# Hybrid mLSTM and attention encoder layer: the input projection and the memory stage become one stage

## The reference, cut to what matters

```
h = rmsnorm(x) * norm_pre
q_m, k_m, v_m, o_m, z_m, if_raw, q_a, k_a, v_a, z_a, g_m, g_a = split(h @ w_in)
for both directions, head by head:              # the memory, as one product over the whole sequence
    b = cumsum(log_sigmoid(f)); a = i - b; m = running max of a (and 0)
    s[t, u] = (q_t . k_u) / 16 * exp(a_u - m_t)  for u up to t (from t on, backwards)
    h_dir[t] = sum_u s[t, u] v_u / max(|sum_u s[t, u]|, exp(-(b + m)_t))
y_m = ((h_fwd + h_bwd) * sigmoid(o_m) * silu(z_m)) @ w_mo
y_a = (attention(rope(q_a), rope(k_a), v_a) * silu(z_a)) @ w_ao
y = rmsnorm(x + (sigmoid(g_m) * y_m + sigmoid(g_a) * y_a) @ w_out) * norm_final
```

## Time and profile before

| | us |
|---|---|
| median of three runs (lowest, highest) | 2832.71 (2832.28, 2835.37) |
| span of the profiled execution, first to last instruction | 2828.9 |
| PE busy, share of the span | 2482.5, 88% |
| DVE, ACT, POOL busy | 1286.5, 884.5, 1064.5 |
| projection's products, gates, memory, all after it | 1265.0, 44.9, 431.9, 1048.1 |

### The profile page before, as it was taken

How to read it: one execution, slowest core, us unless ns; L and a number is a source line. 1 busy time by engine, 2 the same in 40 slices (tenths; PEclk the granted TensorE clock), 3 DMA queues, 4 the chain that set the end, 5 groups by cost and what they waited for, 6 DMA issues and landing times. The chain is left out here.

```text
span 2828.9 us, 31968 instructions
## 1 busy us (share of the span) xinstructions
PE 2482.5 (88%) x11236; PEld 1999.2 (71%) x11236; DVE 1286.5 (45%) x1882; ACT 884.5 (31%) x1564; POOL 1064.5 (38%) x771
## 2 busy tenths in 40 slices
PE   6999999999999999994577776499599888968998
PEld 5888888888888888883455454378477776756887
DVE  6111111112111111103799997489489787862332
ACT  4111111111111111112344332334488776862121
POOL 4111111112211111100567564355377666756320
PEclk9999999999999999997798988699799999998999
DMA  4322222222222222110434332488622323115332
GB/s 157 119 75 75 74 89 75 75 75 89 75 100 78 89 75 75 53 60 20 143 113 151 102 112 89 163 282 281 203 81 81 113 73 97 35 43 204 109 141 90
DMA packets 182207, 299.33 MB, mean 106 GB/s; under 512 B 14864, under 2 KB 72720, under 8 KB 182080
## 3 DMA queue, kind: packets, MB, share of 16 engines
q1 hardware_dynamic: 145520, 225.29, 24.0%
q10 hardware_dynamic: 36560, 72.45, 7.0%
HBM read 190.41 MB, written 107.25 MB: 105 GB/s over the span
## 5 line engine op out<-in xcount | busy, mean ns | idle before, releaser
L148 DVE CAST a_w_hi<-a_raw 128x512 fp32r<-128x512 f32 (+1 forms) x152 | 170.8, 1194 | 995.1 <-PE a_acc L165 995.1
L154 POOL TENSOR_TENSOR a_w_lo<-a_raw,a_w_hi 128x512 fp32r<-128x512 f32 (+1 forms) x160 | 219.6, 1406 | 983.0 <-DVE a_w_hi L148 983.0
L163 PE MATMUL a_acc<-a_act_hi,a_w_hi 128*128 128x512 f32 x1368 | 533.1, 390 | 0.0
L164 PE MATMUL a_acc<-a_act_lo,a_w_hi 128*128 128x512 f32 x1368 | 532.7, 389 | 0.0
L165 PE MATMUL a_acc<-a_act_hi,a_w_lo 128*128 128x512 f32 x1368 | 532.7, 389 | 0.0
L202 ACT ACTIVATE a_stage<-a_acc 128x512 f32<-128x512 f32 x228 | 136.2, 598 | 1081.3 <-PE a_acc L165 1081.3
L1500 POOL TENSOR_TENSOR t_prob<-t_prob,t_rsum 128x1024 f32<-128x1024 f32 (+1 forms) x192 | 308.2, 1609 | 134.8 <-DVE t_rsum L1520 134.8
L164 PEld LDWEIGHTS a_acc<-a_act_lo,a_w_hi 128*128 128x128 f32 x1368 | 257.2, 188 | 53.4
L165 PEld LDWEIGHTS a_acc<-a_act_hi,a_w_lo 128*128 128x128 f32 x1368 | 257.1, 188 | 53.4
L163 PEld LDWEIGHTS a_acc<-a_act_hi,a_w_hi 128*128 128x128 f32 x1368 | 257.3, 188 | 53.1
L1579 PE MATMUL t_scr<-t_k,t_q 128*128 128x512 f32 x640 | 185.0, 404 | 43.8 <-DMA t_k<-stacks 23.8
(11 more groups left out here) (179 smaller groups left out, 4102.8 us busy)
## 6 DMA issues: line engine op xcount, KB each, us to landing
p_feat<-a_stage ACTq DMA_DIRECT2D x42, 1024.0 KB, 4.2
a_raw<-w_in SPq DMA_DIRECT2D x19, 2048.0 KB, 7.7
stacks<-r_flat SPq DMA_DIRECT2D x12, 1536.0 KB, 7.3
p_tok<-a_stage ACTq DMA_DIRECT2D x15, 1024.0 KB, 4.2
m_raw_kq<-p_feat SPq DMA_DIRECT2D x24, 512.0 KB, 5.4
t_q<-stacks SPq DMA_DIRECT2D x8, 1536.0 KB, 6.4
t_k<-stacks SPq DMA_DIRECT2D x16, 768.0 KB, 8.5
r_x<-p_tok SPq DMA_DIRECT2D x12, 768.0 KB, 4.9
```

The source lines that it names most:

```text
L148: nc.vector.tensor_copy(g.w_hi[:, slot, k, 0:width], g.raw[:, k, 0:width]).then_inc(g.hi_split[slot], 1)
L154: nc.gpsimd.tensor_sub(g.w_lo[:, slot, k, 0:width], g.raw[:, k, 0:width], g.w_hi[:, slot, k, 0:width].bitcast(F32)).then_inc(g.lo_split[sl ...
L163: nc.tensor.matmul(out, stat_hi(k), mov_hi(k), start=(k == 0), stop=False)
L164: nc.tensor.matmul(out, stat_hi(k), mov_lo(k), start=False, stop=False)
```

## The change

- The projection keeps the split input in an outer scope and multiplies only 10 blocks of 512 and the gates' block: q and k (4), v (2), attention's q, k, v (3), and one block made of the first head's halves of `o_m` and `z_m`. The gates' work runs inside, between the third to fifth blocks, on five tiles of 128 by 1024, with the two sequences and directions on four groups of partitions.
- q, k and v leave it already split: ACT copies the high part out of PSUM, DVE subtracts for the low part, and both are stored (`kq`, `vs`).
- The other 36 blocks of 128 columns (`o_m` and `z_m` of three heads, `z_a`, `g_m`, `g_a`: 108 groups) are multiplied in the memory's stage, one group every 0.755 tick, from two PSUM tiles. ACT splits their weights (high) and POOL (low), ACT takes them out with Sigmoid or Silu.
- The memory has 80 units in one unrolled order. It loads q, k and v split. A unit's values follow 1.45 ticks after its scores, from weights that are not scaled; the two directions have PSUM sums of their own, and a chunk's numerators are multiplied once by the inverse denominator. The denominator is made as columns (8 matmuls of one column), inverted, and spread by 8 transposes on PE. Three POOL operations end a chunk: add the directions, two gatings.
- A unit in which both directions meet now has values in two pieces of (j+1) and (4-j) blocks of 128 columns, six matmuls each.
- The pre-loaded semaphores of these stages become plain counts, and one setting of the program, the room for dynamic transfers, is made 1024.

The core of the diff (removed lines of the old stages left out; they are printed above):

```diff
-    project(nc, x, w_in, norm_pre, p_feat, p_tok, gate_rows)
-    prepare_gates(nc, gate_rows, b_if, neg_max, floor, a_cols)
-    mlstm(nc, p_feat, p_tok, neg_max, floor, a_cols, scratch("inverse", NDIR * CH), g_mem)
+    project_and_remember(nc, x, w_in, norm_pre, b_if, gate_rows, kq, vs, p_tok, p_feat, neg_max, g_mem)
...
+A_UNITS = [("qk", C_QM, 0), ("if", C_IF, 0), ("qk", C_QM + UNIT, 1), ("qk", C_QM + 2 * UNIT, 2),
+           ("qk", C_QM + 3 * UNIT, 3), ("v", C_VM, 0), ("v", C_VM + UNIT, 1), ("tok", C_QA, S_QA),
+           ("tok", C_QA + UNIT, S_QA + UNIT), ("tok", C_KVA, S_KVA), ("oz", C_OM, 0)]
...
+                    if kinds[idx] in ("qk", "v"):
+                        nc.scalar.activation(stage[:, i % 2, 0, j, :].bitcast(F32R), a[:], ACT.Copy).then_inc(half_made, 1)
...
+                        nc.vector.tensor_sub(stage[:, i % 2, 1, j, :].bitcast(F32R), acc[(G0[idx] + n) % NB][:],
+                                             stage[:, i % 2, 0, j, :]).then_inc(lo_made, 1)
...
+    for u, (_, _, _, j, _) in enumerate(units):
+        at("sp", u - 1.9, "load k", u)
+        at("sp", u - 1.0, "load v", u)
+        if j is not None:
+            at("dve", u - 0.75, "argument", u)
+        at("act", u - 0.6, "decay", u)
+        at("pe", u, "scores", u)
+        at("dve", u + 0.2, "weigh", u)
+        at("pool", u + 0.4, "sum", u)
+        at("act", u + 0.55, "high", u)
+        at("dve", u + 0.65, "low", u)
+        at("pe", u + 1.45, "values", u)
+    for ch in range(len(first)):
+        a, z = first[ch], last[ch]
+        at("sp", a - 2.6, "load q", ch)
+        at("sp", a - 2.5, "load nmax", ch)
+        at("pool", a + 0.35, "zero", ch)
+        at("sp", z - 1.0, "load gates", ch)
+        at("pe", z + 1.25, "den", ch)
+        at("act", z + 1.3, "abs", ch)
+        at("dve", z + 1.4, "invert", ch)
+        at("pe", z + 1.65, "spread", ch)
+        at("act", z + 1.75, "norm", ch)
+        at("dve", z + 1.9, "out", ch)
+        at("pool", z + 2.1, "gate", ch)
+        at("sp", z + 2.6, "store out", ch)
+    for g in range(NG_B):
+        t = -1.0 + g * 0.755 + 0.07
+        at("pe", t, "group", g)
+        at("act", t + 0.6, "drain", g)
+        at("sp", t + 1.0, "store group", g)
+        if g % NCH == 0:
+            i = g // NCH
+            at("sp", t - 2.9, "load w", i)
+            at("act", t - 1.5, "w high", i)
+            at("pool", t - 1.4, "w low", i)
...
+                elif kind == "drain":
+                    act.wait_ge(acc_full, n + 1)
+                    if n >= 3:
+                        act.wait_ge(stored[n % 3], 16 * (n // 3))
+                    nc.scalar.activation(stage[:, n % 3, :], acc[n % 2][:], ZG_SUBS[n // NCH][2]).then_inc(drained, 1)
...
+                    for d, out in ((1, out_f), (0, out_b)):
+                        ins = nc.vector.tensor_mul(out[:], num[d][:], norm[:, d:d + 1, :].to_broadcast([P, 2, CH]))
+                    ins.then_inc(out_read, 1)
...
+                    nc.gpsimd.tensor_add(out_f[:], out_f[:], out_b[:]).then_inc(gate_step, 1)
+                    pool.wait_ge(gate_step, 2 * n + 1)
+                    nc.gpsimd.tensor_mul(out_f[:], out_f[:], gate_o[:]).then_inc(gate_step, 1)
+                    pool.wait_ge(gate_step, 2 * n + 2)
+                    nc.gpsimd.tensor_mul(out_f[:], out_f[:], gate_z[:]).then_inc(out_made, 1)
...
+                if kind == "group":
+                    i, c = n // NCH, n % NCH
+                    if n >= 2:
+                        pe.wait_ge(drained, n - 1)
+                    pe.wait_ge(w_low, i + 1)
...
+                    pe.wait_ge(v_loaded[n % 3], 16 * (n // 3 + 1))
+                    pe.wait_ge(lowed, n + 1)
+                    v, hi, lo = v_t[:, n % 3], wt_hi[:, n % 2], wt_lo[:, n % 2]
+                    for d, of, to in parts(n):
...
-    nc = bacc.Bacc("TRN2", target_bir_lowering=False, num_devices=1)
+    nc = bacc.Bacc("TRN2", target_bir_lowering=False, num_devices=1, dynamic_dma_scratch_size=1024)
```

More of the change, by code:

```diff
@@ L45 @@
 C_GM = C_ZA + W_A
-R_QM, R_OM, R_ZM, R_ZA, R_GM, R_END = 0, 2 * W_M, 3 * W_M, 4 * W_M, 4 * W_M + W_A, 4 * W_M + W_A + 2 * D
-S_QA, S_KVA, S_VM, S_END = 0, W_A, W_A + 2 * W_KV, W_A + 2 * W_KV + W_M
+R_OM, R_ZM, R_ZA, R_GM, R_END = 0, W_M, 2 * W_M, 2 * W_M + W_A, 2 * W_M + W_A + 2 * D
+S_QA, S_KVA, S_VM = 0, W_A, W_A + 2 * W_KV
 UNIT = 512
@@ L79, in sem, with count, counts @@
         return self.used[-1]
+    def count(self, name):
+        self.used.append(self.nc.alloc_semaphore(f"{self.tag}_{name}"))
+        return self.used[-1]
+    def counts(self, name, n):
+        return [self.count(f"{name}{i}") for i in range(n)]
     def sems(self, name, n):
@@ L90, in make_identity @@
                             base=0, pattern=[[-1, P]], channel_multiplier=1).then_inc(sem, 1)
[L93 to L113, removed]
 def over_turns(eng, steps, step, count, ticks):
@@ L135, in over_turns @@
         ticks_of(i)
[L138 to L155, removed]
 def product(nc, pe, out, stat_hi, stat_lo, mov_hi, mov_lo, before_k=None):
@@ L166, in product @@
     return last
[L169 to L191, removed]
@@ L194, in drain_unit @@
[L194 to L206, removed]
@@ L556 @@
-CHUNKS = [(0, 8, 0), (0, 8, 4), (8, 4, 8)]
-BLK = CH // P
-UNITS = sum(n for _, n, _ in CHUNKS)
-FIRST = [sum(m for _, m, _ in CHUNKS[:c]) for c in range(NCH + 1)]
-def units_of_head():
-    return [(c, first + i, (first + i - own if own <= first + i < own + BLK else None), first + i < own)
-            for c, (first, n, own) in enumerate(CHUNKS) for i in range(n)]
-KQ_PIECES = [("k", 0), ("q", 0), ("k", 1), ("q", 1), ("k", 2), ("q", 2)]
-NKQ = len(KQ_PIECES)
-KQ_RING = 3
-TICKS = UNITS
-def head_plan():
+NDIR = 2
@@ new lines, with a_groups, halves_of_a @@
+BLK = CH // P
+HUNIT = UNIT // 2
+A_UNITS = [("qk", C_QM, 0), ("if", C_IF, 0), ("qk", C_QM + UNIT, 1), ("qk", C_QM + 2 * UNIT, 2),
+           ("qk", C_QM + 3 * UNIT, 3), ("v", C_VM, 0), ("v", C_VM + UNIT, 1), ("tok", C_QA, S_QA),
+           ("tok", C_QA + UNIT, S_QA + UNIT), ("tok", C_KVA, S_KVA), ("oz", C_OM, 0)]
+def a_groups(idx):
+    return NCH if A_UNITS[idx][0] == "if" else NG
+G0 = [sum(a_groups(i) for i in range(idx)) for idx in range(len(A_UNITS) + 1)]
+def halves_of_a():
+    out = []
+    for idx in range(len(A_UNITS)):
+        size = NCH if A_UNITS[idx][0] == "if" else 2
+        out += [(idx, list(range(n, n + size))) for n in range(0, a_groups(idx), size)]
+    return out
@@ new lines @@
+GATE_ROWS = 7
+CHUNKS = [(0, [4, 5, 6, 7, 0, 1, 2, 3], 0), (0, [0, 1, 2, 3, 7, 6, 5, 4], 4), (8, [8, 9, 10, 11], 8)]
+WW = CH + P
+ZG_SUBS = [(col + h * DM + b * P, row + h * DM + b * P, func) for h in range(1, HM)
+           for col, row, func in ((C_OM, R_OM, ACT.Sigmoid), (C_ZM, R_ZM, ACT.Silu)) for b in range(DM // P)]
+ZG_SUBS += [(C_ZA + b * P, R_ZA + b * P, ACT.Silu) for b in range(W_A // P)]
+ZG_SUBS += [(C_GM + b * P, R_GM + b * P, ACT.Sigmoid) for b in range(2 * D // P)]
+NG_B = NCH * len(ZG_SUBS)
@@ L581, in head_plan, with memory_units, memory_plan @@
+def memory_units():
+    return [(h, c, s, s - own if own <= s < own + BLK else None, s < own)
+            for h in range(HM) for c, (_, order, own) in enumerate(CHUNKS) for s in order]
+def memory_plan(units, first, last):
     plan = {e: [] for e in ("sp", "pool", "act", "dve", "pe")}
@@ L584, in at @@
         plan[engine].append((tick, kind, n))
-    units = units_of_head()
-    start = [2 + FIRST[c] for c in range(NCH)]
-    end = [1 + FIRST[c + 1] for c in range(NCH)]
-    for n, (c, s, j, _) in enumerate(units):
-        score, value = 2 + n, VALUES_AFTER + n
-        if j is not None:
-            at("dve", score, "argument", n)
-        at("act", score, "decay", n)
-        at("pe", score, "scores", n)
-        at("dve", score + 0.9, "weigh", n)
-        at("pool", score + 1.3, "sum", n)
-        at("dve", value - 1.3, "scale", n)
-        at("act", value - 1.4, "high", n)
-        at("pool" if j is None else "dve", value - 0.6, "low", n)
-        at("pe", value, "values", n)
@@ L601, in head_plan @@
-    for c in range(NCH):
-        at("dve", start[c] - 1.5, "zero", c)
-        for k, (engine, kind) in enumerate((("pe", "den"), ("act", "abs"), ("sp", "move"), ("dve", "invert"),
-                                            ("sp", "keep"), ("sp", "spread"))):
-            at(engine, end[c] + (2.4, 3.1, 3.1, 4.2, 4.3, 4.9)[k], kind, c)
-        out = VALUES_AFTER + FIRST[c + 1] - 1 + 0.4
-        at("dve", out, "gate", c)
-        at("pool", out + 0.5, "gate", c)
-        at("sp", out + 0.7, "store", c)
-        at("sp", (19.5, out - 6.0, out - 2.1)[c], "load gates", c)
-        at("sp", (-5.5, 2.5, 4.5)[c], "load nmax", c)
-        at("sp", (3, 4, 7)[c], "load floor", c)
-        at("act", (14.3, 16.8, 20.8)[c], "v high", c)
-        at("pool", (14.3, 17.8, 21.8)[c], "v low", c)
-        at("sp", (10.7, 14.7, 17.5)[c], "load v", c)
@@ new lines, with project_and_remember @@
```

(13 more changed lines are left out.)

1277 lines of the change are left out of this document (653 added, 624 removed).

## The result

The changed kernel takes 2649.61 us (median of 4 runs, 2648.83 to 2650.65) against 2833.81 for the kernel before (median of 4): a ratio of 0.9351, 95% interval 0.9337 to 0.9364. That is 184 us less. The forecast was 2696 and the range began at 2665, so the direction was right and the gain was a third larger than forecast. The profiled execution took 2650.65 us, with a span of 2648.8.

A forecast was written before the change was run, and what follows sets the result against it. PE was taken to bound the projection and, at 866 us against ACT's 456, the merged stage. Stage terms moved `rotate`'s start from 1780.8 to 1644.3, the span from 2828.9 to 2692.4; plus 3.8, forecast 2696, range 2665 to 2780.

The forecast's parts named there:

- first stage, last product: Projection's end at 718.3 us: start at 38.97, 8.4 of startup, 123 groups in 669.1, gate transposes 1.8.
- to the first merged product: Handover into the merged stage: 7.1 us after the last product, then 11.5 for weight load, rounding and subtraction.
- body of the merged stage: Merged projection and memory work, set by PE: 865.8 us of matmuls, 3 at lower clock, 18 at chunk ends; 886.8.
- `rotate` to the end: Everything after the merged stage, taken as not touched by the change and kept at 1048 us.
- median above the span: The median of the runs was taken to stand 3.8 us above the profile's span.
- chunk ends: Merged stage, PE waiting between denominator and spreading, and for norm copies: 1.5 us each, 18 in all, between 0 and 5 each.
- narrow matmuls: Values in two pieces, below 512 columns: 90.9 us taken, 132.5 if width did not matter; 41.6 put into the range.
- Denominators: Merged stage, 8 per chunk, each as two passes on PE: 21.9 us in all, half of that as the other end.
- 1 (chunk ends, 60 us): Merged stage: POOL's gating or slow DVE arguments make low parts 5 us late per chunk, 60 us, 2756; chance 0.15.
- 2 (transfers set the pace): Merged stage: 124 MB at 134 GB/s take 925 us against PE's 887, giving 2734; chance 0.05.
- 3 (ACT's queue, slower): Merged stage: 163 table loads on ACT delay PE by 210 us, 2906, slower than before; chance 0.10.
- 4: Merged stage: waits of 1.6 to 1.8 us a unit eat just the room, so no change; chance 0.02.

## Why the prediction was right or wrong

Step by step, forecast against the profile after; the differences add up to the 46 us of the miss (2696 less 2649.6).

| step | forecast | measured | difference |
|---|---|---|---|
| first stage, last product | 718.3 | 716.1 | -2.2 |
| to the first merged product | 18.6 | 12.7 | -5.9 |
| body of the merged stage | 886.8 | 872.1 | -14.7 |
| end of the stage | 20.6 | 19.0 | -1.6 |
| `rotate` to the end | 1048.1 | 1029.0 | -19.1 |
| median above the span | 3.8 | 0.8 | -3.0 |

**What failed** is one sentence: "What follows is not touched." The work is not touched, but its price, 1048.1 us, was copied from the old execution as if a stage's time belonged to its instructions alone. In that time were stalls at both turns of the loop, which hung on the length of the code ahead of it. Attention took 510.3 us in place of 531.1, and the kernel before, with its loop moved and nothing else, 510.4. Without these 19 us the time would have been 2668.7, inside the range: some 165 of the 184 us are the change's own work, and 19 came by where its code happened to put the loop. The rows were there to see: the waits of ACT with "issue" as releaser, 10 us each, where ACT's other waits in attention all name what they wait for. These waits without a releaser were no property of the stage, and a change that moves code could take them away (the changed kernel) or bring them back (the same with 170 instructions ahead of the loop).

**The body** was right in its mechanism and over-sized in one term. The chunk ends were put at 18 us, between 0 and 60, and all waits in the body are 1.7 us. The rest of the sum holds: 868 measured (872.1 less those waits and 2.3 for the first 12 matmuls, which start 0.43 apart) against 865.8. The narrow matmuls lie at the lower end, as taken. One unit's values in two pieces of 256 and 384 columns, and the scores behind them:

```profile
1580.12 0.28 PE L953 MATMUL m_num<-m_wt_hi,m_v 128*128 128x256 f32 x1
1580.23 0.28 PE L953 MATMUL m_num<-m_wt_lo,m_v 128*128 128x256 f32 x1
...
1581.53 0.33 PE L953 MATMUL m_num<-m_wt_lo,m_v 128*128 128x384 f32 x1
1581.71 0.33 PE L953 MATMUL m_num<-m_wt_hi,m_v 128*128 128x384 f32 x1
1581.88 0.39 PE L916 MATMUL m_scr<-m_q,m_k 128*128 128x512 f32 x1
```

256 columns start 0.11 to 0.12 apart and 384 columns 0.17 to 0.18; 128 columns, in other units, 0.11, as the prediction took. The unit takes 1.76 us, six times 0.293 against the 0.287 forecast. Denominators cost 1.70 us a chunk (1595.96 to 1597.66), 20.4 in all against 21.9.

**The start and the handover** were sized from far rows. The store that ends the first stage lands in 2.8 us, not 4.2, and the chain from load to product took 7.9 us (720.86 to 728.74) where the next stage's 11.5 stood for it. The first product of the whole kernel also came at 36.6, 2.4 us earlier than before; from there the first stage took 679.5 us against 679.3 forecast. The last row of the table is no cost of the kernel: an execution's time stands 1.7 to 2.0 us above its own span in every run. The 3.8 compared the median of some executions with the span of another, which by that was about 2 us quicker.

**The rivals.** 1 (chunk ends, 60 us): nothing of it; POOL's gating lies under the groups. 2 (transfers set the pace): the stage moves data at 143 GB/s and no wait for a load is among PE's two lines; with the groups moved ahead, 75.9 us for k appear. 3 (ACT's queue, slower): ACT is busy 444 us against 456 forecast, and taking away half of that changes nothing. 4 fell with the result.

## What to carry to other kernels

Work without waits of its own, laid between the steps of a stage that waits, can be worth more than the waits that it fills: here it removed 115 us of waits and another 69 us, of which the lower clock had cost some 55. When a stage is called untouched, look first for waits in it that end with no releaser, above all at a loop's turn; here they belonged to the place of the code, and a few instructions ahead of the loop moved them. To compare two versions whose code differs in length, compare the loops' turns too, or write the loops out.

## What was not expected of the hardware

A turn of a loop of 373 instructions on ACT or 343 on DVE cost nothing or 4.3 to 5.5 us by its place, and 26 instructions on ACT decided it (1247 against 1221). With ACT's stall behind DVE's, 21 us were lost in two turns; with ACT's alone, or beside DVE's, 12 to 13. With the loop written out on both engines, attention is another 4 us shorter than with free turns. In the stretch where PE was busy 348 of 464 us, the granted clock was 0.86 on average; in the stage where it was busy 870 of 872, it was 1.00.
